# MoBA scores in two passes over stacked high and low queries, in place of three passes

## The reference, cut to what matters

```
MLA:  8 heads, q and k of 96 (64 + 32 rotary), v of 64, causal softmax
MoBA: 8 heads, q and k of 64, v of 64, blocks of 256 keys,
      top 3 past blocks by q . mean(k), plus the own block, causal
s = q @ k.T * scale;  p = softmax(masked s);  o = p @ v
h = x + rms_norm(concat(o of both) @ w_out)
h = h + rms_norm(relu(rms_norm(h) @ w_up)^2 @ w_down)
```

## Time and profile before

| | us |
|---|---|
| median of 3 runs | 580.34 (580.08 to 580.38) |
| the profiled execution | 580.28 |
| its span | 578.5 |
| PE busy | 565.6 (98%) |
| DVE busy | 396.2 (68%) |
| ACT busy | 298.8 (52%) |
| POOL busy | 95.6 (17%) |

### The profile page before, as it was taken

How to read it: one execution, slowest core, us unless ns; L and a number is a source line. 1 busy time by engine, 2 the same in 40 slices (tenths; PEclk the granted TensorE clock), 3 DMA queues, 4 the chain that set the end, 5 groups by cost and what they waited for, 6 DMA issues and landing times.

```text
span 578.5 us, 8130 instructions
## 1 busy us (share of the span) xinstructions
PE 565.6 (98%) x2824; PEld 466.2 (81%) x2824; DVE 396.2 (68%) x755; ACT 298.8 (52%) x619; POOL 95.6 (17%) x157
## 2 busy tenths in 40 slices
PE   7999999999999899999999999999999999999995
PEld 7988898877666588898888888888888888888883
DVE  3539573488767237618757757758877988877897
ACT  5573163588876144534353353346255566565461
POOL 1163110355776001200000000000000001000004
PEclk9999999999999999999999999999999999999998
DMA  8451331000022092056778688877986555516503
GB/s 296 147 147 56 125 130 74 0 2 2 1 74 74 1 327 74 1 212 231 288 259 302 231 263 280 285 259 242 363 304 216 167 199 188 194 56 202 162 1 145
DMA packets 42911, 95.15 MB, mean 164 GB/s; under 512 B 3840, under 2 KB 22016, under 8 KB 39552
## 3 DMA queue, kind: packets, MB, share of 16 engines
q1 hardware_dynamic: 41840, 94.74, 47.1%
q10 hardware_dynamic: 1040, 0.00, 0.1%
HBM read 79.01 MB, written 15.73 MB: 164 GB/s over the span
## 4 chain that ended last, share of the span: by engine, by line
PE 97%; DMA 1%; DVE 1%; issue 0%; SPq 0%; POOLq 0%; DVEq 0%; ACT 0%; POOL 0%; ACTq 0%
PE bank L1238 30%; PE bank L1239 29%; PE bank L1240 29%; PE bank L1430 3%; PE bank L1412 3%; DMA x_sb<-in_x 1%; PE bank L1344 1%; PE bank L1244 1%; PE bank L1277 1%; PE bank L1361 0%; DVE uT_lo L820 0%; PE bank L1303 0%; DVE pT L981 0%; POOLq L75 0%; SPq L334 0%
## 5 line engine op out<-in xcount | busy, mean ns | idle before, releaser
L1238 PE MATMUL bank<-uT_hi,w_hi 128*128 128x512 f32 (+1 forms) x280 | 104.1, 372 | 0.0
L1239 PE MATMUL bank<-uT_lo,w_hi 128*128 128x512 f32 (+1 forms) x280 | 103.8, 371 | 0.0
L1240 PE MATMUL bank<-uT_hi,w_lo 128*128 128x512 f32 (+1 forms) x280 | 103.8, 371 | 0.0
L1238 PE MATMUL bank<-w_hi,a_hi 128*128 128x512 f32 x224 | 87.2, 389 | 0.0
L1240 PE MATMUL bank<-w_hi,a_lo 128*128 128x512 f32 x224 | 87.2, 389 | 0.0
L1239 PE MATMUL bank<-w_lo,a_hi 128*128 128x512 f32 x224 | 87.1, 389 | 0.0
L823 DVE SCALAR_TENSOR_TENSOR w_lo<-w_raw,g_up,w_hi 128x256 fp32r<-128x256 f32 x128 | 52.1, 480 | 46.8 <-ACT w_hi L530 46.8
L530 ACT ACTIVATE w_hi<-w_raw,g_up 128x256 fp32r<-128x256 f32 x128 | 53.0, 496 | 44.6 <-PE bank L1240 28.6
L530 ACT ACTIVATE w_hi<-w_raw 128x1024 fp32r<-128x1024 f32 (+2 forms) x49 | 46.7, 993 | 52.2 <-PE bank L1240 48.6
L820 DVE TENSOR_TENSOR w_lo<-w_raw,w_hi 128x1024 fp32r<-128x1024 f32 (+1 forms) x41 | 49.0, 1235 | 23.2 <-ACT w_hi L530 23.1
L1238 PE MATMUL bank<-w_hi,uT_hi 128*128 128x512 f32 (+1 forms) x160 | 62.1, 388 | 0.0
(11 more groups left out here) (150 smaller groups left out, 946.3 us busy)
## 6 DMA issues: line engine op xcount, KB each, us to landing
stage<-in_w_down SPq DMA_DIRECT2D x17, 1024.0 KB, 5.0
w_raw<-in_w_up SPq DMA_DIRECT2D x16, 1024.0 KB, 8.3
pair_sums<-stage SPq DMA_DIRECT2D x13, 1024.0 KB, 10.0
w_raw<-in_w_down SPq DMA_DIRECT2D x10, 1024.0 KB, 6.5
w_raw<-pair_sums SPq DMA_DIRECT2D x10, 1024.0 KB, 4.8
w_raw<-in_w_in SPq DMA_DIRECT2D x6, 1024.0 KB, 5.4
w_raw<-in_w_out SPq DMA_DIRECT2D x4, 1024.0 KB, 4.9
stage<-pair_sums SPq DMA_DIRECT2D x3, 1024.0 KB, 4.7
```

The costliest lines, as they stand in the source:

```text
L1238: nc.tensor.matmul(out, lh, rh, start=start, stop=False)
L1239: nc.tensor.matmul(out, lh, rl, start=False, stop=False)
L1240: return nc.tensor.matmul(out, ll, rh, start=False, stop=stop)
```

## The change

Four edits. The scores of MoBA heads use a stationary tile of 128 rows, with the 64 rows of the head's high query part above the 64 rows of its low part, and a moving tile in which the same 64 rows of keys stand twice, once for the high and once for the low part of k. Two matmuls then give all four products, the low x low one too. The stacked tiles (`q_stack`, `k_hi2`, `k_lo2`, two buffers each, both heads of a pair side by side) are written by 12 DMAs per pair inside SBUF, issued by SP, each of 64 rows of 512 elements. PE waits for all 12 ahead of a pair's scores. And the preparation of q for MoBA pairs comes a round earlier: for head 8 between the first and the other score tiles of head 7, for the later ones in odd rounds. SP's output weight chunks 2 and 3 are issued behind the copies of heads 12 and 14.

```
+        q_stack, k_hi2, k_lo2 = [[sb(f"{n}{j}", [P, 2, S], F32R, stack=att) for j in range(2)] for n in (...)]
...  SP
-            for i, r in enumerate(OUT_CH):
-                chunk(r, w_out_v[:, 2 * i:2 * i + 2, :], CW)
+            def stack(m):
+                s, d = slot(2 * m), m % 2
+                halves = (slice(0, MOBA_D), slice(MOBA_D, P))
+                def copies(tile, parts):
+                    for h in range(2):
+                        for n in range(2):
+                            sp.dma_start(tile[halves[n], h, :].bitcast(F32), parts[n][halves[h], :].bitcast(F32)).then_inc(stacked, 16)
+                if m >= HEADS // 2 + 2:
+                    sp.wait_ge(s_full, 3 * (2 * m - 2))
+                sp.wait_ge(ql, preps(2 * m))
+                copies(q_stack[d], (qT_hi[s], qT_lo[s]))
+                sp.wait_ge(kl, preps(2 * m))
+                copies(k_hi2[d], (kT_hi[s], kT_hi[s]))
+                copies(k_lo2[d], (kT_lo[s], kT_lo[s]))
+            out_chunk(0)
+            out_chunk(1)
+            for m in range(HEADS // 2, HEADS):
+                stack(m)
+                if m >= HEADS - 2:
+                    out_chunk(m - HEADS + 4)
...  ACT loop
                 if i >= 2:
                     p_part(i - 1, 0)
+                if i == HEADS - 2:
+                    q_part(HEADS)
                 k_part(i + 2)
...
-                q_part(i + 2)
+                if i + 2 < HEADS:
+                    q_part(i + 2)
                 if i + 1 < NH:
                     exps(i + 1, S_ORDER[1:])
+                if i + 3 > HEADS:
+                    q_part(i + 3)
...  DVE loop
                 if i >= 2:
                     p_part(i - 1, 1)
+                if i == HEADS - 2:
+                    q_part(HEADS)
                 if i + 1 < NH:
                     maxes(i + 1, S_ORDER[:1])
...
                     maxes(i + 1, S_ORDER[1:])
-                q_part(i + 2)
+                if i + 2 < HEADS:
+                    q_part(i + 2)
+                if i + 3 > HEADS:
+                    q_part(i + 3)
...  PE, q_prep
+                    elif i == HEADS:
+                        pe.wait_ge(p5_ready, HEADS - 3)
+                        pe.wait_ge(ql, preps(HEADS - 1))
                     elif i >= 3:
-                        pe.wait_ge(p5_ready, i - 2)
+                        pe.wait_ge(p5_ready, i - 2 if i < HEADS else i - 3)
...  PE, scores
+                elif 0 in tiles:
+                    pe.wait_ge(stacked, 16 * 12 * (i // 2 - HEADS // 2 + 1))
...
+                    else:
+                        d, h = i // 2 % 2, i % 2
+                        nc.tensor.matmul(ps[b][:, c:c + w], q_stack[d][:, h, tok], k_hi2[d][:, h, 0:w], start=True, stop=False)
+                        last = nc.tensor.matmul(ps[b][:, c:c + w], q_stack[d][:, h, tok], k_lo2[d][:, h, 0:w],
+                                                start=False, stop=True)
...  PE, probs_T
-                        pe.wait_ge(ql, preps(max(j for j in range(min(i + 3, NH)) if prepared(j))))
+                        pe.wait_ge(ql, preps(i + 2 if i < HEADS - 3 else HEADS if i < HEADS - 1 else min((i - 1) // 2 * 2 + 4, NH - 2)))
...  PE loop
-                if 2 <= i <= NH:
+                if i == HEADS - 2:
+                    q_prep(HEADS)
+                elif 2 <= i <= NH:
                     probs_T(i - 1, PT_ORDER[3:])
                 if i + 1 < NH:
                     scores(i + 1, (1, 2, 3))
-                q_prep(i + 2)
+                if i == HEADS - 2:
+                    probs_T(i - 1, PT_ORDER[3:])
+                if i + 2 < HEADS:
+                    q_prep(i + 2)
+                elif i + 3 > HEADS:
+                    q_prep(i + 3)
```

More of the change, by code:

```diff
@@ L135, in build @@
         pT = [sb(f"pT{i}", [P, TRI], stack=att) for i in range(4)]
+        q_stack, k_hi2, k_lo2 = [[sb(f"{n}{j}", [P, 2, S], F32R, stack=att) for j in range(2)] for n in ("q_stack", "k_hi_twice", "k_lo_twice")]
         att.close()
@@ L197, in build @@
         kT_full, kh, kl = sem("kT_full"), sem("kh"), sem("kl")
+        stacked = sem("stacked")
         s_full, s_nb, s_exp = sem("s_full"), sem("s_nb"), sem("s_exp")
@@ L351, in _, with out_chunk @@
             in_chunk(7)
-            for i, r in enumerate(OUT_CH):
-                chunk(r, w_out_v[:, 2 * i:2 * i + 2, :], CW)
+            def out_chunk(i):
+                chunk(OUT_CH[i], w_out_v[:, 2 * i:2 * i + 2, :], CW)
+            def stack(m):
[18 more added lines that the diff above has]
+                    out_chunk(m - HEADS + 4)
             sp.wait_ge(o_full, NH // 2)
@@ L1364, in scores @@
             def scores(i, tiles=range(NT)):
-                if 0 in tiles:
+                s, r = slot(i), slice(0, QH)
+                if 0 in tiles and i < HEADS:
                     pe.wait_ge(kl, 2 if i == 0 else preps(i))
                     pe.wait_ge(ql, preps(i))
-                s, r = slot(i), slice(0, QH)
-                if i >= HEADS:
-                    r = slice(MOBA_D * (i % 2), MOBA_D * (i % 2) + MOBA_D)
+                elif 0 in tiles:
+                    pe.wait_ge(stacked, 16 * 12 * (i // 2 - HEADS // 2 + 1))
                 for n in tiles:
@@ L1376, in scores @@
                     w, tok = P * (t + 1), slice(P * t, P * t + P)
-                    last = mm3(ps[b][:, c:c + w], qT_hi[s][r, tok], qT_lo[s][r, tok], kT_hi[s][r, 0:w], kT_lo[s][r, 0:w],
-                               True, True)
+                    if i < HEADS:
+                        last = mm3(ps[b][:, c:c + w], qT_hi[s][r, tok], qT_lo[s][r, tok], kT_hi[s][r, 0:w], kT_lo[s][r, 0:w],
+                                   True, True)
+                    else:
[3 more added lines that the diff above has]
+                                                start=False, stop=True)
                     if n != 2:
```

## The result

| | us |
|---|---|
| changed kernel, median of 4 runs | 603.5 (602.33 to 604.68) |
| kernel before | 580.32 (580.08 to 580.38) |
| ratio | 1.040, 95% interval 1.038 to 1.042 |
| profiled execution of the changed kernel | 602.33, span 600.5 |

Slower, as forecast, but by 23.2 us and not 11.7: outside the range of 585 to 599.

The account below looks back on a forecast made before the run. TensorE was taken as the bound, busy for 98% of the span. Pace and landing of copies less savings, 32p + 4L - 12.15, gave +9.9, with the clock +11.4 us; on 580.28 that is 592 us, range 585 to 599.

Parts of the forecast that it names:

- first pair's start: Scores of heads 8, 9: PE waits for the last of twelve copies, landing at 149.2 instead of 144.92; stall 4.3 us.
- three periods: Start to start of successive MoBA pairs: 13.3 us instead of 10.93, each 2.4 us longer, 7.1 in all.
- after the last pair's start: Last two heads: 2.5 us of PE work saved, of which 1.4 us gain was taken, between 0 and 2.5.
- the clock: PE's first work after each of four stalls at half speed: 0.4 us each, 1.5 in all, bounds 0 and 5.
- the pace of 0.44 us a copy: SP's time per issue of a stacking copy, taken from a burst of four h_sb loads; bounds 0.33 to 0.64.
- The formula: Time difference for pace p and landing L, before the clock: 32p + 4L - 12.15, +9.9 for 0.44 and 2.0.
- The rival with half-rate copies (598): Data on half the partitions, not the issue, sets the pace: 0.64 us a copy, 6.4 us more, 598 us; chance 0.22.
- Landing 2.0: Time from the last copy's issue until it lands: 2.0 us, as for 256 KB stores; bounds 1.4 to 2.6.
- The q copies have long been issued: SP's queue in later pairs: q copies out before low k is ready, so eight k copies follow it, 5.1 us.
- S: Start of a pair's first scores after a stall; next pair's low q ends at S + 5.66, low k S + 8.2.
- PE's saving: MoBA heads on PE: third pass 0.58 and 64/128-row changes 0.67, together 1.25 us per head, 10.0 for eight.
- the moved weight chunks at no cost: Two output weight chunks behind the stacking in SP's queue: cover of more than 8 us, so no cost.

Follow-up runs that it names:

- warm_wide: Changed kernel with PE kept busy in its four waits for the copies by 26 (later 20) matmuls of 512 columns: 599.55 us, 1.033.
- full_rows: Changed kernel with 6 copies of 128 rows per pair instead of 12 of 64, same bytes, MoBA's stacking left out: 587.21 us, 1.012.
- p2_r128: Kernel before with MoBA scores in two passes on 128 rows of the pair's tiles as they are, no copies or stacking: 575.60 us, 0.9924.
- zero_pad: Kernel before with each MoBA head's queries in a 128-row tile, other 64 rows zero, three passes kept: 578.92 us, 0.9976.

## Why the prediction was wrong

The spans as a ledger, with the prediction's own steps:

| step | forecast | at full clock (warm_wide) | changed kernel |
|---|---|---|---|
| first pair's start | +4.3 | +6.8 | +6.9 |
| three periods | +7.1 | +13.6 | +15.0 |
| after the last pair's start | -1.4 | -1.5 | +0.2 |
| the clock | +1.5 | (0) | (in the rows above: 3.1) |
| sum | +11.4 | +18.9 | +22.0 |

(The column sums hold to 0.1; 22.0 and 18.9 are the differences of the spans. In the medians the clock is 3.95.)

**The step that failed: the pace of 0.44 us a copy.** It came from the burst of HBM loads; a copy from SBUF to SBUF costs SP 0.64 in a row of them. That alone is 32 x 0.20 = 6.4 us of the 11.5 that were missing. The formula held: with p = 0.64 and L = 2.3 it gives 20.5 + 9.2 - 12.15 = +17.5 against +18.9 at full clock, and for the first pair 142.36 + 7.04 + 2.3 = 151.7, where 151.72 and 151.78 were measured. I had the value at the edge of my bounds (0.33 to 0.64) and took the row that looked most alike instead of leaving the middle: the multiplier of 32 made this the term to be careful with.

**The rival with half-rate copies (598) had the size and the wrong reason.** Its pace was 0.64, but half the bytes left the pace as it was. The rate itself: 64 rows moved 205 GB/s at a busy share of 0.88, 128 rows 403 at 1.04 (full_rows), so per busy share 233 against 388. The Trainium skill, "SBUF — State Buffer", section "Door 1: The DMA port swizzle", has half the ports for half the partitions and 218 GB/s; the trace agrees in kind, with a ratio of 0.60. By the measured rates the bytes would set the pace only if an issue cost less than 128 KB / 233 GB/s = 0.56 us.

**Landing 2.0:** 2.3 for 128 KB, 1.2 us over four pairs; 64 KB land in 2.0, 256 KB in 2.4.

**"The q copies have long been issued": wrong.** Low q was forecast at S + 5.66, and the first q copy leaves at S + 5.5 at full clock (157.25 - 151.72). Low k was forecast at S + 8.2 and is there at S + 7.3 to 8.0 in warm_wide, so DVE's chain was estimated well. But with issues of 0.64 us, and one of 1.38 in the first period, the first k copy leaves only at S + 8.7, 8.5 and 8.4: it queues behind the q copies on SP. With the landings this makes the three periods 1.5 us longer at full clock than the formula with the right pace gives. In the changed kernel the low clock delays low q and low k themselves (low k at S + 9.1, 8.5 and 9.0), which makes the periods 1.3 us longer again; there only heads 12, 13 still queue, for 0.3 us.

**The clock, 1.5 forecast, 3.1 to 4.0 measured.** The stalls were longer than I had, but the error is in what the lower clock delays. I counted the scores and half a microsecond of transposes; in fact PE worked at 0.50 from the start of the pair to about 157, and low q, ACT's copy and the probabilities all wait for that PE work (low q starts at S + 5.6 and not 4.8: 157.41 - 151.78, against 156.53 - 151.72 in warm_wide). More than half of the 3.1, 1.7 us, fell on the last pair, where it ate the whole gain: 12.16 us from 199.52 to 211.68 against 10.48 at full clock.

**Right:** PE's saving (1.17 of 1.25 us per head) and both its causes, if by some luck: the third pass is worth 0.64 and not 0.58, the changes between 64 and 128 rows 0.63 and not 0.67, and the new change from 128-row scores to 64-column values, at 0.09, was not in the sum. Right too: that the copies stall PE four times; that no engine's busy time is the limit; the gain after the last pair's start, at full clock (1.5 for 1.4); the moved weight chunks at no cost (388.8 us for the rest, as before). Not said, and shown by p2_r128: with free stacking too only 4.7 of the 10 us would have come through.

## What to carry to other kernels

Count the DMA instructions that a stage waits for, and price each with a row of the same kind; without such a row take the far bound when the count is large. On a path where one engine waits, moving the same bytes in half as many copies halves the time of issue (here 16.3 us of 23.2). Where PE stays idle for microseconds ahead of dependent work, look whether the work behind the stall is slow as well, as it was here, and count what it delays on other engines; and when PE leads by a little only, ask how much of its saving the next engine's chain lets through before paying for it.

## What the runs showed of the hardware

- An issue of a copy inside SBUF takes SP 0.60 us (0.64 from one to the next) for 64 KB and for 128 KB, and 0.55 to 0.69 for 256 KB on 128 rows; the HBM loads took 0.44 and the stores 0.33. It is not the kind of transfer alone: in the changed kernel the same 1 MB weight load took SP 0.59 us right behind the copies (at 181.75) and 0.38 after a pause (at 198.03). What makes the difference stays open; issuing from a second queue wasn't tried.
- Narrow matmuls in a dense row stretched SP's issues beside them from 2.5 to 4.0 us for four; wide ones did not (2.53). One issue of 1.38 us in that run came at 158.39, ahead of the fillers.
- After narrow fillers and 2.12 and 2.24 us without work the clock went to 0.50 once PE's real work had begun; in the same run it stayed at 1.00 after 2.41 and 2.62 us. After wide fillers and waits of 0.4 to 1.44 us it stayed at 1.00 every time.
- Zeros in the unused 64 rows make a 64-row product run like a 128-row one between 128-row transposes: the block takes 3.01 us in zero_pad (149.11 to 152.12), 0.63 less than before.
- A 384-column pass on 128 rows takes 0.18 us to the next start when a transpose follows and 0.27 when a matmul with a 64-column tile follows.
